# Moving a chunk's column sums into the middle of a product unit, and its bias behind the vector engine's work of the position

## The reference, cut to what matters

```python
def reference(x, c, w_mod, b_mod, norm_gain, w_attn_in, ...):      # x: 256 x 2048, two layers
    cond = jax.nn.silu(c)
    for l in range(DEPTH):
        mod = cond @ w_mod[l] + b_mod[l]                 # 2048 -> 12288: six vectors of 2048
        sh1, sc1, g1, sh2, sc2, g2 = jnp.split(mod, N_MOD, axis=-1)
        h = modulate(rms_norm(x, norm_gain[l, 0]), sh1, sc1)
        y = attention_mixer(...) if l % 2 == 0 else pool_mixer(...)
        x = x + g1[:, None, :] * y
        h = modulate(rms_norm(x, norm_gain[l, 1]), sh2, sc2)
        x = x + g2[:, None, :] * conv_ffn(h, w_up[l], conv_w[l], conv_b[l], w_down[l])
    return rms_norm(x, final_gain)
```

## Time and profile before

| what | value |
|---|---|
| time, median of 3 runs | 2108.9 us (2106.12 to 2110.2) |
| the profiled execution's own time | 2114.62 us |
| its span | 2113.0 us |
| PE busy | 2038.8 us, 96% |
| DVE busy | 1633.6 us, 77% |
| ACT busy | 1008.7 us, 48% |
| mean granted TensorE clock | 0.988 |

### The profile page before, as it was taken

How to read it: one execution, slowest core, us unless ns; L and a number is a source line. 1 busy time by engine, 2 the same in 40 slices (tenths; PEclk the granted TensorE clock), 3 DMA queues, 4 the chain that set the end, 5 groups by cost and what they waited for, 6 DMA issues and landing times.

```text
span 2113.0 us, 36723 instructions
## 1 busy us (share of the span) xinstructions
PE 2038.8 (96%) x13730; PEld 1883.5 (89%) x13730; DVE 1633.6 (77%) x2279; ACT 1008.7 (48%) x1345; POOL 307.2 (15%) x459
## 2 busy tenths in 40 slices
PE   2999999999999999999999999899999999999998
PEld 2887989887999989999899987799988999889987
DVE  5677888887899998898989987888865566555565
ACT  3221765454645544555445455554443454434453
POOL 3223342210022122211211210011000000000000
PEclk9999999999999999999999999999999999999999
DMA  9898999886689899898998884387755555555552
GB/s 354 309 343 294 318 311 328 296 296 237 241 312 324 325 343 341 317 330 299 336 348 311 313 295 140 112 322 261 260 182 199 180 179 179 198 188 171 199 179 100
DMA packets 235842, 558.28 MB, mean 264 GB/s; under 512 B 14024, under 2 KB 15032, under 8 KB 235192
## 3 DMA queue, kind: packets, MB, share of 16 engines
q1 hardware_dynamic: 180408, 355.03, 48.4%
q0 software_dynamic: 55296, 201.35, 26.8%
HBM read 554.23 MB, written 2.10 MB: 263 GB/s over the span
## 4 chain that ended last, share of the span: by engine, by line
PE 88%; DVE 5%; issue 2%; ACT 2%; DMA 1%; SPq 0%; DVEq 0%; ACTq 0%; POOLq 0%
PE ps L634 17%; PE ps L636 17%; PE ps L635 17%; PE ps L660 10%; PE ps L662 10%; PE ps L661 10%; PE ps L680 3%; PE ps L698 2%; PE ps L677 1%; DVE w_lo L1359 1%; DVE macc L1373 1%; DMA work<-in_conv_b 1%; ACT work L1024 1%; ACT w_hi L1024 1%; DVE work L1438 1%
## 5 line engine op out<-in xcount | busy, mean ns | idle before, releaser
L1024 ACT ACTIVATE w_hi<-raw 128x1024 fp32r<-128x1024 f32 x640 | 666.7, 1056 | 793.9 <-PE ps L636 488.5
L1359 DVE TENSOR_TENSOR w_lo<-raw,w_hi 128x1024 fp32r<-128x1024 f32 x640 | 766.3, 1224 | 354.0 <-ACT w_hi L1024 353.5
L634 PE MATMUL ps<-h_hi,w_hi 128*128 128x256 f32 x3200 | 914.4, 286 | 1.6 <-DVE w_lo L1359 1.5
L635 PE MATMUL ps<-h_lo,w_hi 128*128 128x256 f32 x3200 | 907.6, 284 | 0.0
L636 PE MATMUL ps<-h_hi,w_lo 128*128 128x256 f32 x3200 | 907.5, 284 | 0.0
L634 PEld LDWEIGHTS ps<-h_hi,w_hi 128*128 128x128 f32 x3200 | 616.5, 193 | 5.0 <-issue 4.7
L635 PEld LDWEIGHTS ps<-h_lo,w_hi 128*128 128x128 f32 x3200 | 616.8, 193 | 2.1 <-issue 1.9
L636 PEld LDWEIGHTS ps<-h_hi,w_lo 128*128 128x128 f32 x3200 | 616.4, 193 | 0.0
L1373 DVE SCALAR_TENSOR_TENSOR macc<-mraw,cond,macc 128x512 f32<-128x512 f32 x620 | 427.5, 746 | 43.0 <-DMA mraw<-in_w_mod 36.9
L519 POOL DMA_DIRECT2D mraw<-in_w_mod x358 | 259.8, 726 | 1191.3 <-DVE macc L1373 866.6
L660 PE MATMUL ps<-w_hi,g_hi 128*128 128x512 f32 x832 | 326.1, 392 | 1.3 <-DVE w_lo L1359 1.3
(11 more groups left out here) (164 smaller groups left out, 1145.1 us busy)
## 6 DMA issues: line engine op xcount, KB each, us to landing
mraw<-in_w_mod POOLq DMA_DIRECT2D x358, 512.0 KB, 6.4
raw<-in_w_up SPq DMA_DIRECT2D x176, 1024.0 KB, 6.0
raw<-in_w_down SPq DMA_DIRECT2D x88, 1024.0 KB, 5.4
raw<-in_w_attn_in SPq DMA_DIRECT2D x48, 1024.0 KB, 8.4
raw<-in_w_attn_out SPq DMA_DIRECT2D x16, 1024.0 KB, 7.1
work<-in_w_mod POOLq DMA_DIRECT2D x12, 512.0 KB, 6.7
early<-in_w_mod POOLq DMA_DIRECT2D x8, 512.0 KB, 15.4
raw<-in_w_pool SPq DMA_DIRECT2D x4, 1024.0 KB, 5.4
```

What stands on the lines that cost most here:

```text
L634: mm(o, wh, ah, start=st, stop=False, skip_group_check=True)
L635: mm(o, wh, al, start=False, stop=False, skip_group_check=True)
L1024: return nc.scalar.activation(o, i, f, **kw)
L1359: V.tensor_tensor(w_lo[:, s, :, :], raw[:, j % 4, h * 1024:(h + 1) * 1024].rearrange("p (k n) -> p k n", k=2), w_hi[:, s, :, :].bitcast(F3 ...
```

## The change

Of the sums at positions 24 and later, PE no longer does them ahead of the unit but between its two halves. A new function `sum_in(pos)` holds the call, and `unit` and `unit_tok` call it when they come to their second half. At positions before 24 it is called ahead of the unit as before. On DVE the bias of such a chunk goes from ahead of the pieces to the end of the position: behind the pieces, the split of unit p+2 and `attention_ends`. `MODS`, `MOD_SUM` and all waits of `mod_sum`, `mod_bias` and `head_out` stay what they were. No instruction is added or removed.

```diff
-            def unit(q, j, k0, first, last, act_hi, act_lo, g2, h_need=None):
+            def unit(q, j, k0, first, last, act_hi, act_lo, g2, h_need=None, sum_at=None):
                 for h in range(2):
                     if h_need is not None:
                         pe.wait_ge(hlo_ready, h_need + k0 + 2 * h + 2)
+                    if h and sum_at is not None:
+                        sum_in(sum_at)
                     sub(q, j, h, k0 + 2 * h, last and h == 1, first and h == 0, act_hi, act_lo, g2)
...
+            def sum_in(pos):
+
                 if mod_sum_at(pos) is not None:
                     ch = mod_sum_at(pos)
                     mod_sum(ch, (ch + 1) % 2, o_before(pos))
...
                 attention_steps(pos)
+                if pos < START:
+                    sum_in(pos)
                 (start_unit if pos < START else qkv_product)(pos)
...
                 attention_steps(pos)
-                if mod_sum_at(pos) is not None:
+                if mod_sum_at(pos) is not None and pos < START:
                     mod_bias(mod_sum_at(pos), 0, mod_sum_at(pos))
                 for ch, j in mod_at(pos):
                     piece(ch, j, (ch + 1) % 2)
                 if START - 3 <= pos + 2 < 65:
                     split((pos + 2) // 4, (pos + 2) % 4)
                 attention_ends(pos)
+                if mod_sum_at(pos) is not None and pos >= START:
+                    mod_bias(mod_sum_at(pos), 0, mod_sum_at(pos))
```

More of the change, by code:

```diff
@@ L642, in unit, with unit_tok @@
                         pe.wait_ge(hlo_ready, h_need + k0 + 2 * h + 2)
+                    if h and sum_at is not None:
+                        sum_in(sum_at)
                     sub(q, j, h, k0 + 2 * h, last and h == 1, first and h == 0, act_hi, act_lo, g2)
-            def unit_tok(q, j, k0, first, last, act_hi, act_lo, g2, h_need=None):
+            def unit_tok(q, j, k0, first, last, act_hi, act_lo, g2, h_need=None, sum_at=None):
                 for h in range(2):
+                    if h and sum_at is not None:
+                        sum_in(sum_at)
                     if h_need is not None:
@@ L865, in qkv_product @@
                 if kind == "v":
-                    unit_tok(pos // 4, pos % 4, 4 * ks, ks == 0, ks == 3, h_hi, h_lo, g % 2)
+                    unit_tok(pos // 4, pos % 4, 4 * ks, ks == 0, ks == 3, h_hi, h_lo, g % 2, sum_at=pos)
                 else:
-                    unit(pos // 4, pos % 4, 4 * ks, ks == 0, ks == 3, h_hi, h_lo, g % 2)
+                    unit(pos // 4, pos % 4, 4 * ks, ks == 0, ks == 3, h_hi, h_lo, g % 2, sum_at=pos)
             def start_unit(pos):
@@ L911, in _ @@
                 pe.wait_ge(o_lo, 4 * (ks + 1))
-                unit_tok(QUAD_OUT + n // 4, n % 4, 4 * ks, ks == 0, ks == 3, g_hi, g_lo, cg % 2)
+                unit_tok(QUAD_OUT + n // 4, n % 4, 4 * ks, ks == 0, ks == 3, g_hi, g_lo, cg % 2, sum_at=pos)
             group_slot_free(G_OUT + 5)
```

## The result

The changed kernel takes 2129.99 us (median of 4 runs, 2128.14 to 2133.32), the kernel before 2109.47 (4 runs, 2106.12 to 2110.2). The ratio is 1.0091 with a 95% interval of 1.0076 to 1.0107: 16 to 23 us slower, 0.9%. The prediction was 2127, from 2114 to 2134, and slower with a chance of 0.88.

What follows compares the result with a forecast made beforehand. PE, busy 96% of the span, was taken as the bound. Terms: -8.3 gain + 0.6 matmul change + 17.9 waits + 8.0 clock = +18.2 us, so 2132.8 profiled, 2127 on the median; range 2114 to 2134.

Steps and rivals of the forecast that it cites:

- The waits: PE's head output at positions 32, 36, 39, 47 waits for the late bias: 7.3, 3.5, 3.0, 4.1, together 17.9 us.
- The clock: PE's clock falls behind each of the four new waits: 2.0 us each, 8.0 us, bounds 0 and 2.5 each.
- The gain taken away: PE's waits at the sums of positions 31, 35, 38 go: 5.0, 0.3 and 3.0 us, 8.3 us gained.
- Rival 3: Biases are there when PE's head output asks, so only the gain is left: -7.7 us, 2101; chance 0.06.
- The second change of matmul kind: A sum amid PE's unit adds a change between matmul kinds: 0 to 0.08 us for 8 sums, taken as 0.6.
- Position 34: The sum at position 35 asks for the bias of 34 in its own middle, when it is just there.
- Rival 4: Delays feed one another, further waits at positions 33 to 38 add up to 8 us: +26, 2135; chance 0.14.
- rival 2: DVE catches up while PE stands, each wait only its least: +1.5 us, 2110, up to 6 more; chance 0.08.
- The time: Whole kernel: +18.2 us, 2132.8 for a profiled execution and 2127 on the median.
- inner range: The forecast's own span of 2122 to 2131 us, by the clock (1.5 to 2.5 each) and position 39.

Runs made afterwards that it cites:

- the four singles: Sums in the middle, all biases ahead but that of position 31, 35, 38 or 46, one per kernel: 2113.84, 2114.03, 2115.08 and 2113.56 us.
- the four early: The changed kernel with the bias back ahead of the pieces at positions 31, 35, 38 and 46, the other seven last: 2108.50 us.
- the sums ahead: Against the changed kernel, sums back ahead of the unit, all biases still at the end of the position: 2134.75 us.

## Why the prediction was right, point by point

- **The waits.** 7.3, 3.5, 3.0 and 4.1 us were predicted at positions 32, 36, 39 and 47, and 7.1, 3.9, 3.6 and 4.2 measured: 17.9 and 18.7 in sum. That they are the cause is shown by the four singles, and by the kernel with all biases ahead, which has the sums in the same place and no loss.
- **The clock.** 8.0 us were predicted and 7.3 measured, as 1.5, 1.4, 1.6 and 2.8, where I took 2.0 for each. The middle of two rows gave the sum and not the parts; that the sum came so near was luck. By the windows above, 3.2, 3.0, 3.4 and 5.7 us of the four positions passed at 1.2 GHz, and the lost 1.5, 1.4, 1.6 and 2.8 are 46, 48, 47 and 48% of them. The Trainium skill (TensorE: Matmul & The Clock Gate, Terms) prices slow time at half its length. Here the trace agrees with the rule to within a tenth. The length of the slow time was the uncertain factor. The prediction read only 37% from unit 31 of the kernel before, "since a part of those passed in the wait". That reading was wrong:

```profile
277.00:278.90 1.90, 0.16 (x2) 0.00 (x1) 1.04 (x4) 1.37 (x3) 0.34 (x1) 1.00 0.88 330
278.90:280.40 1.50, 1.47 (x9) 1.50 (x9) 1.50 (x3) 1.32 (x2) 0.00 (x0) 0.60 0.78 228
280.40:288.70 8.30, 8.30 (x50) 8.30 (x51) 8.00 (x12) 2.29 (x3) 5.99 (x23) 0.66 0.90 306
```

  The wait had a clock of 1.00. The slow time began with the sum, 1.2 us of it, and the unit had 5.6 us, of which the lost 2.5 are 44%.
- **The gain taken away.** The sums' waits are gone, as worked out. The largest part of the 8.3 us can be read in the changed kernel itself: position 32 begins 51.6 us into the stage (279.89 - 228.28), and began 56.7 us into it before (288.69 - 232.04), 5.0 less. But I added the gain of position 31 and the whole wait of 32 as if they were two things. They are one: PE goes on when DVE allows, so there the gain was worth nothing. The sum came out right, since both entered it with their full size.
- **Rival 3's price was wrong.** Without the late biases I gave -7.7 us; the stage shows -5.4, and the two timed comparisons -5.9 and -3.5. The step that failed is that each removed wait is gained whole. PE's lead at position 31 ran into two next waits, 0.9 us for the bias and 1.4 us for the release with `g_lo`. From one position's start to the next, in that kernel against the one before, position 31 is 5.0 us shorter, 35 is 0.4 and 38 is 3.3: 8.7 saved. Positions 32 and 33 are 2.8 us longer together, 16.4 (280.69 to 297.09) against 13.6. The second change of matmul kind was taken at 0.6 us, its upper bound; positions 27, 34, 42, 46 and 49, where nothing else changes, are 0.3 us longer together. That makes 8.7 - 2.8 - 0.3 = 5.6, against 5.4 for the stage.
- **Position 34.** I wrote that the sum of 35 comes just when the bias of 34 is there. In the changed kernel it does, and nothing is waited for. But that is close: with the four early it waits 1.0 us, with the sums ahead 2.6.
- **Rivals 2 and 4.** Rival 4 had the sign wrong: late outputs don't pile up. What rival 2 describes, DVE catching up while PE stands, does happen, against what I wrote there; but it takes 0.8, 2.0 and 0.6 us from the waits at 36, 39 and 47 (the singles against the changed kernel), and not the whole of them.
- **The time.** Predicted +18.2 us against the profile's stage of +18.3. So near a match is partly luck, since the waits came out 0.8 us longer and the clock 0.7 us cheaper. The forecast's inner range of 2122 to 2131 is also wider than its terms give: 1.5 to 2.5 us of clock each and 2.6 to 3.7 us at position 39 make 2125 to 2130. The medians give +20.5, with an interval of 16 to 23. The 2 us between are inside it, and no run here settles them.

## What to carry to other kernels

Before an instruction is moved down its engine's queue, ask who waits for the semaphore that it posts and where that stands in the waiter's order, and then what the things are that it now stands behind. Here one of them waited for the end of the very unit after which the result was needed, so the wait could be foretold from the order alone, and its length from the two timelines laid beside each other. Where a wait is taken away, look for what is late next before its length is booked as a gain: here about a third of it (2.8 of 8.7 us) came back within two positions.

The version that beats both kernels is half of the change: sums in the middle, biases ahead, 0.2 to 0.3% faster than before in two comparisons.

## What the runs showed of the hardware

The clock's price isn't proportional to the wait. Behind 7.1 us of standing still, 1.5 us were lost; behind 4.2 us, 2.8; behind 5.6 us, 2.8; and in the kernel before, 1.5 us behind a wait of 1.5. What counts is how much of the slow time falls on work. In the longest wait of the changed kernel the clock fell while PE stood, and the 3.5 us at 1.2 GHz that passed there cost nothing:

```profile
280.80:287.70 6.90, 0.00 (x0) 0.00 (x0) 6.71 (x9) 6.01 (x9) 5.82 (x13) 0.75 0.88 311
```

In the kernel with all biases ahead, waits of 1.2, 0.9 and 1.4 us left the granted clock of the whole stage at 1.00:

```profile
229.00:508.00 279.00, 270.77 (x1688) 243.91 (x1687) 239.88 (x365) 160.63 (x246) 77.42 (x129) 1.00 0.89 310
```

The waits of 1.8 and 1.5 us in the kernel before, which brought the clock down, differ from these in more than length: a sum of one-column matmuls followed them, where a head output or suffix sums followed the others. No run here parts the two.
